# A hybrid attention and expert layer: another dense pair of token tiles, output additions on VectorE, a row ring for the tail

## The reference

```python
o = jnp.concatenate([_rms(o_a, g_out_a), _rms(o_b, g_out_b)], axis=-1) @ w_out
x = x + gt1 * _rms(o, g_post1)
h2 = _rms(x, g_pre2) * (1 + sc2) + sh2
x = x + gt2 * _rms(_peer(h2, ...), g_post2)

def one(hb):                                   # the experts, per block of tokens
    q = (hb @ w_query).reshape(PEER_BLOCK, PEER_HEADS, 2, KEY_HALF)
    s1, s2 = ...                               # scores against two sets of 128 keys
    v1, i1 = lax.top_k(s1, PEER_TOPK)          # 16 best of each, then 16 best sums
    ...
    gate = jax.nn.softmax(best, axis=-1)
    ug = jnp.take(u_tab, idx, axis=0)          # 16,384 experts of 1,024 numbers
    vg = jnp.take(v_tab, idx, axis=0)
    act = jax.nn.gelu(jnp.einsum('td,thkd->thk', hb, ug), approximate=False)
    return jnp.einsum('thk,thkd->td', (gate * act), vg)
```

## Time and profile before

| | us |
|---|---|
| median of 3 runs (lowest, highest) | 3762.18 (3758.28, 3764.04) |
| profiled execution | 3763.87 |
| its span | 3762.1 |
| DVE busy | 2257.7 (60%) |
| PE busy | 2965.3 (79%) |
| POOL busy | 1903.5 (51%) |
| u gathers, issue on POOL (L1726, 1,088) | 1029.4 |
| v gathers, issue on POOL (L1742, 832) | 788.4 |

### The profile page before, as it was taken

One profiled execution on the slowest core, in us unless ns is written; L12 is line 12 of the kernel. 1 busy time (PEld: TensorE's weight loads), 2 busy tenths in 40 slices (PEclk: granted clock), 3 DMA queues, 4 the chain that ended last, 5 costly groups with the idle time before them and its releaser, 6 DMA issues.

```text
span 3762.1 us, 28882 instructions
## 1 busy us (share of the span) xinstructions
PE 2965.3 (79%) x8352; PEld 1059.7 (28%) x8352; DVE 2257.7 (60%) x6080; ACT 948.4 (25%) x1848; POOL 1903.5 (51%) x1964
## 2 busy tenths in 40 slices
PE   8999894967757786646877466666767999999898
PEld 2454453431212222201222111122123433333222
DVE  3102624888898986657666877788788766520000
ACT  1001631235575562201111101243153000000100
POOL 0000402346757775556566677767774455531465
PEclk9999897978979998879999799988998999999999
DMA  9300432789989998799899999999999999975898
GB/s 348 112 24 25 139 121 79 256 295 410 411 311 406 418 406 314 276 399 419 330 359 376 365 419 419 419 396 419 419 419 360 410 383 395 384 281 191 299 372 332
DMA packets 367262, 1214.87 MB, mean 323 GB/s; under 512 B 43670, under 2 KB 71574, under 8 KB 363898
## 3 DMA queue, kind: packets, MB, share of 16 engines
q0 software_dynamic: 276640, 1006.79, 68.7%
q1 hardware_dynamic: 74192, 176.49, 12.6%
q10 hardware_dynamic: 16272, 29.74, 2.2%
HBM read 1182.08 MB, written 30.79 MB: 322 GB/s over the span
## 4 chain that ended last, share of the span: by engine, by line
PE 29%; DMA 23%; DVE 12%; POOL 10%; issue 7%; ACT 2%; SPq 0%; ACTq 0%; DVEq 0%; POOLq 0%
DMA mem<-in_u_tab,idx 14%; PE ps_y L2237 12%; DMA mem<-in_v_tab,idxT 7%; DVE mem L2129 6%; POOL mem L1726 5%; POOL mem L1742 5%; PE ps_g L2260 5%; PE ps_y L2260 3%; PE ps_h L2260 3%; PE ps_y L2184 3%; PE ps_y L1163 1%; DMA mem<-h_d 1%; PE ps_y L689 1%; DVE mem L2112 1%; DVE mem L754 0%
## 5 line engine op out<-in xcount | busy, mean ns | idle before, releaser
L2129 DVE CUSTOM_DVE_ANT_0 mem<-mem,ps_h 128x1024 f32<-128x1024 f32 x1088 | 1322.9, 1216 | 574.5 <-DMA mem<-in_u_tab,idx 554.9
L1726 POOL DMA_INDIRECT mem<-in_u_tab,idx x1088 | 1029.4, 946 | 610.2 <-DVE mem L2129 387.3
L2260 PE MATMUL ps_y<-mem 128*32 128x512 f32 x2304 | 955.3, 657 | 423.8 <-DMA mem<-in_v_tab,idxT 350.9
L1742 POOL DMA_INDIRECT mem<-in_v_tab,idxT x832 | 788.4, 948 | 593.1 <-PE ps_g L2260 266.8
L2260 PEld LDWEIGHTS ps_y<-mem 128*32 128x32 f32 x2304 | 189.3, 116 | 1107.5 <-issue 582.7
L2237 PE MATMUL ps_y<-mem 128*128 128x512 f32 x1024 | 466.3, 604 | 2.2 <-DVE mem L2099 2.2
L2237 PEld LDWEIGHTS ps_y<-mem 128*128 128x128 f32 x1024 | 188.2, 191 | 279.1 <-issue 279.1
L2093 DVE TENSOR_SCALAR mem<-mem 128x1 f32<-128x1 f32 (+1 forms) x9 | 1.3, 144 | 385.8 <-ACT mem L1932 385.8
L2260 PE MATMUL ps_g<-mem 128*32 128x512 f32 x512 | 221.1, 618 | 11.4 <-DMA mem<-in_v_tab,idxT 11.4
L2184 PE MATMUL ps_y<-mem 128*128 128x512 f32 x512 | 228.7, 603 | 1.4 <-ACT mem L2006 1.4
L550 PE MATMUL ps_z<-mem 128*128 128x512 f32 (+1 forms) x576 | 190.4, 491 | 4.6 <-DVE mem L468 4.6
(11 more groups left out here) (233 smaller groups left out, 3269.8 us busy)
## 6 DMA issues: line engine op xcount, KB each, us to landing
mem<-in_v_tab SPq DMA_DIRECT2D x128, 512.0 KB, 6.6
mem<-in_w_ada SPq DMA_DIRECT2D x12, 2048.0 KB, 12.3
mem<-in_u_tab,idx POOLq DMA_INDIRECT x1088, 7.7
mem<-in_w_query SPq DMA_DIRECT2D x16, 1024.0 KB, 16.6
mem<-in_v_tab,idxT POOLq DMA_INDIRECT x832, 7.5
mem<-in_w_in SPq DMA_DIRECT2D x8, 1024.0 KB, 17.8
mem<-in_w_out SPq DMA_DIRECT2D x16, 512.0 KB, 8.8
s_d<-mem SPq DMA_DIRECT2D x16, 512.0 KB
```

Of the source, the lines that this page charges most:

```text
L1726: nc.gpsimd.indirect_dma_start(urow[s % RU][:, :], None, A["u_tab"][:, :], bass.IndirectOffsetOnAxis(ap=places[:, col:col + 1], axis=0)).t ...
L1742: nc.gpsimd.indirect_dma_start(vrow[v % RV][:, :], None, A["v_tab"][:, :], bass.IndirectOffsetOnAxis(ap=idxT[n % 2][:, t:t + 1], axis=0)). ...
L2129: nc.vector.tensor_tensor_reduce(out=urow[s % RU][:, :], in0=urow[s % RU][:, :], in1=ps_h[:, :], scale=1.0, scalar=0.0, op0=ALU.mult, op1= ...
L2260: last = nc.tensor.matmul(sums(n)[r, f], W[:, b, 31 - a:63 - a], vrow[v % RV][:, f], start=(a == 0), stop=(a == 31), skip_group_check=True)
```

## The change

Five things are edited. (1) The dense pair is tiles 4 and 5; items are tiles 0 to 3, the 128 blocks, then tiles 6, 7 and 8; the due table has 676 items in the loop in place of 736, the blocks from slot 780 to 994. The slots of finishing, one-hots and attention (every 7 slots) follow. (2) After the last slot (`TAIL`) gathers go round eleven rows, `vrow` and `urow`. (3) The output's two additions for tiles 5 to 8 are DVE's, right behind `residual` and `second`; tiles begin at slot 298, and the steps are spread anew. (4) Queries and scores are steps of their own within the unit (`round_step`). (5) Places of sums and waits that follow from this; the reload of `w_query` doesn't wait for a finished tile.

```diff
-PAIRS = ((5, 6),)
+PAIRS = ((4, 5),)
...
-    def add_residual(self, pool, t):
+    def add_residual(self, eng, math, t):
...
-        self.nc.gpsimd.tensor_tensor(x[0:rows, :], x[0:rows, :], self.ot[t % 2][0:rows, :], ALU.add)\
+        eng.wait_ge(self.x_full[t % 2], self.stored(t))
+        eng.wait_ge(self.o_scaled, t + 1)
+        math.tensor_tensor(x[0:rows, :], x[0:rows, :], self.ot[t % 2][0:rows, :], ALU.add)\
...
+    ITEMS = [x for n in range(4) for x in tokens(n)] + blocks(0) + [x for n in (6, 7, 8) for x in tokens(n)]
...
-    DUE = [(0, 0), (74, 0), (166, 64), (198, 64), (378, 192), (382, 192), (560, 320), (594, 320), (748, 448), (752, 448),
-           (892, 576), (914, 576), (966, 616), (NU, 736)]
+    DUE = [(0, 0), (80, 0), (200, 64), (206, 64), (395, 192), (397, 192), (590, 320), (596, 320), (766, 448), (780, 448),
+           (994, 576), (996, 576), (NU, 676)]
...
-    BURST = {5: (712, 3), 6: (840, 2)}
+    BURST = {4: (598, 3), 5: (712, 2)}
...
-    EVAC = {170: 0, 381: 1, 563: 2}
-    NORM = {198: 0, 384: 1, 584: 2, 752: 3, 896: 4}
-    FINISH = {206: 0, 392: 1, 592: 2, 760: 3, 903: 4}
-    STORE = {212: 0, 398: 1, 598: 2, 766: 3, 908: 4}
-    GATE = {2: 0, 3: 1, 5: 2, 6: 3, 7: 4, 8: 5}
-    H2_AFTER = {216: 3, 402: 4, 602: 6, 770: 7, 912: 8}
...
-    ATT_AT = {68 + 8 * p: att.BACK + 2 * p for p in range((att.ALL - att.BACK) // 2)}
+    EVAC = {203: 0, 398: 1, 593: 2}
+    NORM = {207: 0, 402: 1, 597: 2, 769: 3, 998: 4, 1016: 5}
+    FINISH = {216: 0, 412: 1, 607: 2, 778: 3, 1008: 4, 1026: 5}
+    STORE = {222: 0, 418: 1, 613: 2, 784: 3, 1012: 4, 1030: 5}
...
+    GATE = {2: 0, 3: 1, 5: 2, 6: 3, 8: 4}
+    H2_AFTER = {226: 3, 422: 4, 617: 6, 788: 7}
...
+    ATT_AT = {68 + 7 * p: att.BACK + 2 * p for p in range((att.ALL - att.BACK) // 2)}
     A_SCORE, A_LOGS, A_SOFT, A_AFTER, A_WEIGHTS, A_FINISH, A_VALUES, A_READ = 0, 1, 3, 4, 5, 6, 7, 8
-    OUT_AT = {328 + 14 * i: NT // 2 + 1 + i for i in range(NT // 2)}
+    OUT_AT = {298 + 14 * i: NT // 2 + 1 + i for i in range(NT // 2)}
...
+    PRIOR = {2: 0, 3: 1, 6: 2, 7: 3, 8: 6}
...
-        ysum = [mem.at(G0_AT + 15 * D, D), mem.at(G0_AT + 15 * D, D), mem.at(OB_AT + 2 * D, D)]
+        ysum = [mem.at(G0_AT + 15 * D, D), mem.at(OB_AT + 3 * D, D), mem.at(OB_AT + 2 * D, D)]
...
-            return urow[n - 6] if n >= 6 else io
+            return mem.at(G0_AT + D * (n - 6), D) if n >= 6 else io
...
-            return {4: ps_y[1], 6: ps_y[1], 7: ps_g, 8: ps_h}.get(n, ps_y[0])
-        BEFORE = {5: 3, 6: 4}
+            return {5: ps_y[1], 6: ps_g, 8: ps_y[1]}.get(n, ps_y[0])
+        BEFORE = {4: 3, 5: 2, 7: 4, 8: 5}
...
-        full, uses = {}, {}
+        TAIL = due(NU - 1)
+        def row(v):
+            p = (v - TAIL) % (RU + RV)
+            return v % RV if v < TAIL else (TAIL + p) % RV if p < RV else RV + (NU + p - RV) % RU
+        def wait_row(eng, v):
+            if v < TAIL + RV:
+                if v >= RV:
+                    eng.wait_ge(v_used, v - RV + 1)
+            elif v < TAIL + RV + RU:
+                eng.wait_ge(u_used, NU - RU + (v - TAIL - RV) + 1)
+            else:
+                eng.wait_ge(v_used, v - RV - RU + 1)
+        rows = vrow + urow
+        row_full = v_full + u_full
+        full, uses = {}, {("v", RV + i): len(range(i, NU, RU)) for i in range(RU)}
         for v, (n, a, b) in enumerate(ITEMS):
-            kind = ("b" if n is None else "v", v % RV)
+            kind = ("b" if n is None else "v", row(v))
...
+        def round_step(q, k):
+            if round_at(q) is not None:
+                return {0: {0: 0, 3: 1, 5: 2}, LATE: {1: 0, 6: 1, 11: 2}}[UNITS[q][0]].get(k)
...
-            sp.wait_ge(y_done, 2)
...
-                    sp.wait_ge(v_used, v - RV + 1)
-                    sp.dma_start(vrow[v % RV][:, :], A["v_tab"][c * NKEY:(c + 1) * NKEY, :])\
-                        .then_inc(block_full[v % RV], 16)
+                    wait_row(sp, v)
+                    sp.dma_start(rows[row(v)][:, :], A["v_tab"][c * NKEY:(c + 1) * NKEY, :])\
+                        .then_inc(block_full[row(v)], 16)
...
-                if v >= RV:
-                    pool.wait_ge(v_used, v - RV + 1)
-                elif v == 0:
+                wait_row(pool, v)
+                if v == 0:
...
                 nc.gpsimd.indirect_dma_start(
-                    vrow[v % RV][:, :], None, A["v_tab"][:, :],
-                    bass.IndirectOffsetOnAxis(ap=idxT[n % 2][:, t:t + 1], axis=0)).then_inc(v_full[v % RV], 16)
+                    rows[row(v)][:, :], None, A["v_tab"][:, :],
+                    bass.IndirectOffsetOnAxis(ap=idxT[n % 2][:, t:t + 1], axis=0)).then_inc(row_full[row(v)], 16)
...
-                    for t, step in outs(s):
-                        if step == 12:
-                            out.add_residual(pool, t)
-                        elif step == 17:
-                            out.add_second(pool, t)
...
+                    if n in PRIOR:
+                        act.wait_ge(W_ready, 32 * (gathered.index(PRIOR[n]) + 1))
...
+                if n == 1:
+                    act.wait_ge(out.ab_done, 2 * len(out.tiles))
...
-                    elif step == 2:
+                    elif step == 3:
                         out.branch_roots(act, own, t)
-                    elif step == 4:
+                    elif step == 6:
                         out.scaled_half(act, t, 0)
-                    elif step == 7:
+                    elif step == 11:
                         out.scaled_half(act, t, 1)
-                    elif step == 9:
+                    elif step == 14:
                         out.branch_end(act, own, t)
-                    elif step == 14:
+                    elif step == 17:
                         out.residual_root(act, own, t)
...
-                    copy_q(z, 0)
-                    if h:
-                        copy_scores(z - 1)
-                    copy_q(z, 1)
-                elif round_at(q - 1) is not None:
-                    copy_scores(round_at(q - 1))
...
+                    if round_step(q, k) in (0, 1):
+                        copy_q(z, round_step(q, k))
+                    elif round_step(q, k) == 2:
+                        copy_scores(z)
...
-            take_w(NT)
             for v in items(NU):
+                if v == end[6]:
+                    take_w(NT)
                 if ITEMS[v][0] is not None:
                     put_w(v)
-                if v == end[5] + 8:
-                    norm(5)
-                elif v == end[5] + 16:
-                    store(5)
-                    norm(6)
-                elif v == end[5] + 24:
-                    store(6)
-                elif v == end[7] + 8:
-                    norm(7)
-                elif v == end[7] + 20:
-                    store(7)
+                for n in (6, 7):
+                    if v == end[n] + 8:
+                        norm(n)
+                    elif v == end[n] + 24:
+                        store(n)
...
-                    if step == 3:
+                    if step == 4:
                         out.branch_norms(dve, own, t)
-                    elif step == 5:
+                    elif step == 8:
                         out.product(dve, t, 0)
-                    elif step == 8:
+                    elif step == 13:
                         out.product(dve, t, 1)
-                    elif step == 10:
+                    elif step == 16:
                         out.residual(dve, own, t)
-                    elif step == 15:
+                        out.add_residual(dve, nc.vector, t)
+                    elif step == 19:
                         out.second(dve, own, t)
+                        out.add_second(dve, nc.vector, t)
...
-                    if s - 2 in T_SLOT and T_SLOT[s - 2] not in dense:
-                        take_idx(T_SLOT[s - 2])
+                    if s - 6 in T_SLOT and T_SLOT[s - 6] not in dense:
+                        take_idx(T_SLOT[s - 6])
...
-                    pe.wait_ge(att.o_read, 3 * FA)
+                    pe.wait_ge(out.ab_rs, len(out.tiles))
...
-                        elif n == 4:
-                            pe.wait_ge(q_copied, 4 * PH)
-                        elif n == 7:
+                        elif n == 6:
                             pe.wait_ge(g_evac, groups(dense[-1], NGRP))
-                            pe.wait_ge(t_copied, n + 1)
-                            pe.wait_ge(i_copied, placed(n))
-                        elif n == 8:
-                            pe.wait_ge(t_copied, n + 1)
-                            pe.wait_ge(i_copied, placed(n))
+                            pe.wait_ge(t_copied, NT)
+                            pe.wait_ge(i_copied, placed(7))
+                        elif n in BEFORE:
+                            pe.wait_ge(y_done, BEFORE[n] + 1)
...
-                            pe.wait_ge(t_copied, 3)
-                            pe.wait_ge(i_copied, 3)
```

(27 more changed lines are left out.)

36 lines of the change are left out of this document (14 added, 22 removed).

## The result

The changed kernel takes 3540.3 us (median of four runs, 3538.5 to 3548.1) against 3760.2 us for the kernel before beside it: ratio 0.9419 [0.9401, 0.9436]. The forecast was 3550 us with a range of 3490 to 3640. The profiled execution took 3539.1 us, its span is 3537.3 us.

A forecast was written before the change was run, and what follows sets the result against it. Transfers at 419 GB/s were taken as the bound, with four stretches short of it through POOL waits, PE lumps, PE's blocks and the tail. Sum: 658 + 155 + 502 + 400 + 298 + 290 + 630 + 246 + 371 = 3550 us; range 3490 to 3640.

The forecast's parts named there:

- the four stretches: Short of 419 GB/s: output tiles (POOL waits), second half's queries (PE lumps), slot 914 on (PE), tail (mainly six rows).
- Slots 0 to 63: First slots, 158 us before: query and score steps bring little since DVE is busy; 155 (bounds 150 and 160).
- Slots 64 to 291: 518 us before: nine items fewer, four attention steps more, DVE 467 us at 93% busy; 502 (bounds 490 and 518).
- Slots 292 to 447: Output tiles, 438 us before: POOL loses eight additions and their waits; 400 (bounds 376 and 438).
- the first rival (3588): DVE stands where POOL stood, so slots 292 to 447 stay at 438 us; whole 3588, chance 0.14.
- The contention of 0 to 8 us: Output tiles: eight moved additions on DVE may hold gathers beside them, 0 to 8 us, inside the 400.
- Slots 448 to 575 and 576 to 703: Second half's queries in steps, 326 to 298 us (bounds 285 and 326); then 290 us unchanged (bounds 285 and 300).
- Slots 704 to 995: 701 us before, 59 items go; beside blocks transfers 430, PE 440, slots 445 at 2.06 each; 630 (bounds 610 and 670).
- The tail: After the loop, 427 us before: 284 gathers through eleven rows, paced by POOL and transfers, plus 12 us at the end; 371.
- the second rival (3617): The ring does not slow the tail; 1.49 us a gather is PE's or transfers' pace: tail 438, whole 3617, chance 0.12.
- all at the transfers' rate: Every stretch from slot 64 on runs 1% over its bytes, 2270 in place of 2366 us; whole 3454, chance 0.10.
- The order of items: Rival: new order gives back in the tail what the loop gains; only additions (38) and queries (28) count; 3696, chance 0.07.

The follow-up runs named there:

- after: The changed kernel itself with all five edits, as profiled, against the kernel before: 3540.3 us, ratio 0.9419.

## Why the prediction came out as it did

**The bounds of the four stretches were read rightly.** Three of these losses came back, each when its part alone was undone: the output tiles' POOL waits (39 us), the lump's wait for v rows (29 us) and the six-row tail (37 us). The fourth, PE behind from slot 914 on, was not undone in any run: the largest share, 80.6 us, rests on the traces, where PE was behind before and is now busy for 440 of 442 us beside the blocks.

**Slots 0 to 63: wrong sign.** The step that failed is "DVE is busy 144 of the 158 us, so little can come". It looked at what could come, not at what the spread steps put in front: ACT's copies of the scores ahead of the gelu, 13.3 us of DVE's wait against 9.1. 163.2 lies over the upper bound of 160. In the whole this costs little, since the lump loses in the next stretch most of what it gives here.

**Slots 64 to 291: the 93%.** DVE's work was forecast at 467 us and measured 464.4. The busy share rose from 88 to 90%, not to 93. "With the transfers eased" failed: an item still costs some 0.9 us there (17 more items, 15.9 us), so nine fewer items paid for four more attention steps and no more. That these cost some 9 us is borne out (9.2 when undone). Why both DVE and the transfers fall short together is not settled: with six u rows POOL's wait for a dot falls from 100.8 to 91.0 us, but with five v rows its wait for PE rises from 4.1 to 11.2 us, and the stretch stays. A sixth u row beside six v rows was not run.

**Slots 292 to 447: mechanism right, the allowances too large.** The tiles' slots 298 to 358 took 154.4 us, 2.53 a slot, for 2.6 forecast. In them DVE is busy for 131.9 us, 2.16 a slot and not 2.36; the transfers move 389 GB/s. The other 95 slots took 229.0 us for 241: the 21 from 359 to 379 with the reload 68.4, and the last 68 2.15 each for 2.2 forecast, so at that pace the reload and the restart cost some 25 us and not 32. DVE's output steps, one or two slots behind ACT's, wait for at most 1.3 us. POOL does wait in these slots, 52.4 us for rows that a dot has to free; the sign "no wait of POOL" holds for the additions alone. So the first rival (3588) fell: in the changed kernel the chain is no shorter, but its waits end before the step is due.

**The contention of 0 to 8 us: gathers are held by some 5 us, nearly all of it beside the operation that DVE had before.** In after a gather beside the pair on DVE takes up to 1.91 us, as before:

```profile
1396.06 1.28 DVE L1253 SCALAR_TENSOR_TENSOR mem<-mem 128x1024 f32<-128x1024 f32 x1
1396.24 1.91 POOL L1762 DMA_INDIRECT mem<-in_v_tab,idxT  x1 [0.30 <-issue]
1397.38 1.23 DVE L1268 TENSOR_TENSOR mem<-mem 128x1024 f32<-128x1024 f32 x1
```

With the additions on POOL and far off, the same line of DVE with no addition behind it:

```profile
1458.99 1.28 DVE L1253 SCALAR_TENSOR_TENSOR mem<-mem 128x1024 f32<-128x1024 f32 x1
1459.28 1.80 POOL L1762 DMA_INDIRECT mem<-in_v_tab,idxT  x1 [0.30 <-issue]
1460.19 1.21 DVE L2147 CUSTOM_DVE_ANT_0 mem<-mem,ps_h 128x1024 f32<-128x1024 f32 x1
```

Both gathers end 2.09 us after that instruction began, 0.81 us after its end, with the `tensor_tensor` behind it and without. In after seven gathers are held so in the output tiles, 1.25 to 1.91 us each in place of 0.94, 4.6 us together.

A `tensor_tensor` alone holds them too, as one of 128x512 with both inputs in SBUF does in the first token tile:

```profile
670.19 0.69 DVE L1041 TENSOR_TENSOR mem<-mem,const 128x512 f32<-128x512 f32 x1
670.33 1.36 POOL L1747 DMA_INDIRECT mem<-in_u_tab,idx  x1 [1.52 <-DVE mem L2144]
```

That gather ends 0.81 us after the `tensor_tensor` as well. In after's loop all 39 gathers that began at least 0.1 us into a `tensor_tensor` of this kind (longer than 0.25 us), and more than 0.2 us before its end, end 0.81 or 0.82 us after it. The Trainium skill (SBUF — State Buffer, "Who interferes with whom") infers that a `tensor_tensor` does not hold up descriptors; this trace does not agree (1.36 us for the gather above in place of 0.94), and the measurement decides. Of the two rules that the prediction set side by side, the first, on two SBUF inputs, fits these rows, but not its price of 8 us. The additions could hold gathers, then, but they follow right behind an operation that does. A gather held by that one runs on into the addition, and the next begins near the addition's end:

```profile
1387.81 1.23 DVE L1262 TENSOR_TENSOR mem<-mem 128x1024 f32<-128x1024 f32 x1
1388.83 1.02 POOL L1762 DMA_INDIRECT mem<-in_v_tab,idxT  x1 [0.30 <-issue]
```

Three gathers take 1.02 or 1.03 us so, some 0.3 us in all: that is what the moved additions hold. Whether the stretch is longer for any of this was not measured.

**Slots 448 to 575 and 576 to 703: right,** 291.7 for 298 and 285.2 for 290. One v gather still waited 8.9 us, under the 10 that I had set as the sign.

**Slots 704 to 995: 621.1 for 630, but one reason was wrong.** The clock of 1.00 and PE's 440 us held (0.99; 440.03). The floor of 2.06 us a slot did not: it was read from 32 slots with a finish in them, and bare slots go at 1.69 us. It did no harm because PE's 440 stood beside it. The 14 slots without items took 33.7 us for 29: token tile 3's `NORM` and `FINISH` are due in them (769, 778), as the diff had shown.

**The tail: 377.6 for 371.** The gathers came as forecast: from the last gather's issue at 3514.66 to the end are 22.7 us, so they took 354.9 for 359. The 12 us "from the last row to the end" were mis-sized: 12.3 us from the last gather's issue to the table load at 3526.99 and 10.3 behind it. The 10.2 us from the table load on the earlier trace rows were only the second of the two, and I had put some 2 us for the first. The ring was what slowed the tail, against the second rival (3617), but six rows without pairs go at 1.41 us, not 1.49. The counts of items are one or two off (98 and not 100 in the last stretch, 286 and not 284 behind it), which moves no term by more than 3 us.

**The errors offset.** Forecast too short were 8 us (slots 0 to 63), 15 (64 to 291), 5 (766 to 779) and 7 (tail), 34 in all; forecast too long were 17 (292 to 447), 6, 5, 5 (704 to 765), 9 (780 to 995), 4 and 2 (the start), 47. Of the rivals, "all at the transfers' rate" came nearest from below: from slot 292 to 1087 it is nearly what happened (1824 us for 1795), and the stretch 64 to 291, 516.5 for 475, makes half of the 86 us by which it misses the whole. That 3540 came so close to 3550 is in part luck, since errors of 34 and 47 us offset each other. The order of items gave nothing back in the tail, since 60 gathers more there cost 1.2555 us each and the pairs were gone.

## What to carry to other kernels

An instruction that waits at the head of the queue which issues the gathers costs its wait, not its work: move it to where its input is surely ready, or to an engine that comes to it in the same order as its input; which engine does it mattered little here. When one stretch has spare time on an engine and another is full, spread the plain work so that each slot needs about the same of transfers, PE and DVE, and after a change look for a bunch: a faster engine can make one. A floor read from a stretch holds only for what was in that stretch: list its instructions before using it elsewhere.

## What the runs showed of the hardware

- With half of PE's work in the blocks' stretch the kernel got 27.7 us slower there: blocks 2.5 us apart at 419 GB/s, then bare slots of 1.69 us at 324 GB/s.
- A gather that POOL issued while DVE ran a `tensor_tensor` or a `scalar_tensor_tensor` with both inputs in SBUF was held until 0.81 or 0.82 us after that operation's end: in after all 39 beside a `tensor_tensor` of more than 0.25 us and all 9 beside a `scalar_tensor_tensor` of 1,024 columns that began at least 0.1 us into it and more than 0.2 us before its end (up to 1.91 us in place of 0.94). Of those that began within 0.02 us of the operation's start none was held, and none of 20 beside such an operation with an input in PSUM, nor of 556 beside a dot.
- POOL issued gathers of 128 rows every 1.2555 us for 280 gathers in a row. Their 512 KB take 1.251 us at 419 GB/s, and one issue with its gap 1.24 us: for this size the two nearly coincide, and these runs don't tell which sets the pace.
